# Turning the next stage's first half inside the stage before it, and a feed-forward pipeline that lags by two chunks

## The chip, the cores and the metric

The kernel runs on one core of a Trainium2 chip. The metric is the device time of one launch in microseconds; smaller is better. Float32 data throughout.

## The reference, cut to what matters

256 tokens with 1024 columns go through two blocks and a third part. In each block `h = h + 0.5 * swiglu(rms_norm(h))`, a mixer (attention in two forms in the first block, forgetting attention in the second), a second feed-forward, and a gate:

```python
def swiglu(x, w_gate_up, w_down):
    g, u = jnp.split(x @ w_gate_up, 2, axis=-1)
    return (jax.nn.silu(g) * u) @ w_down
...
    gate = jax.nn.sigmoid(rms_norm(h, ple_norm[i]) @ ple_w_gate[i])
    h = h + gate * (p[i] @ ple_w_proj[i])
```

The third part is block attention and spatial gating, a cross attention on a memory, and a feed-forward over product keys ("peer"), each a norm followed by a product. Every stage thus reads the whole of the `h` that the stage before it has just finished.

## The kernel before, in words

**Arithmetic.** A float32 product is made of three fp32r products, high times high, high times low and low times high (`product`, L248; its matmuls are L250, L251, L252). A stage's input is turned by TensorE (transposes, L255), the high part is cut off the PSUM result by ScalarE (`x_hi`, L277) and the low part by VectorE (`x_lo`, L286, or L289 without a gain). The weights come as 340 units of 1 MB in the order in which they are used (`load_unit`, L223, three places in `raw`, `w_hi` and `w_lo`); ScalarE makes `w_hi` (`split_hi`, L235) and VectorE `w_lo` (`split_lo`, L240). A unit is 24 matmuls of 512 columns: four chunks of 128 rows, two tiles of tokens, three products.

**Order.** There are no queues or planners: each engine runs a program written out by hand (`tensor_program`, L2098, and its siblings), with semaphores between them. An engine works strictly in its order. `split_hi(u + LEAD)` and `split_lo(u + LEAD)` stand beside the use of unit `u`, with LEAD = 2. `split_hi(u)` must wait until TensorE has used unit `u - 3`.

**Stages** are ffa0, mix0 (`tensor_even`), ffb0, ple0, ffa1, mix1 (`tensor_odd`), ffb1, ple1, moba (up to its product out2), cross, peer. The halves below are halves of the 1024 columns of `h`, for all 256 tokens: half 0 is chunks 0 to 3, half 1 chunks 4 to 7. A stage begins like this (`tensor_normed`, `scalar_normed`, `vector_normed`, L319 on):

- TensorE waits for half 0 of `h`, makes 8 transposes, ScalarE makes 4 `x_hi`, VectorE 4 `x_lo`, and the first product waits for the first two of these.
- VectorE adds half 1 of `h` only after these four `x_lo` (the closure `finish`, returned by the stage before: L534 after a feed-forward, L384 after a mixer, L595 and L598 after ple).
- TensorE uses the stage's first unit for token tile 0 (12 matmuls), makes the 8 transposes of half 1, and goes on with token tile 1.
- ScalarE squares all of `h` (L304), POOL makes the root (L314), and only then ScalarE splits the next unit but one.

**A feed-forward** (`tensor_ffn`, L445) has 11 chunks of 256 hidden columns. Of each chunk come two units of first product (`tensor_up`), silu (L476) and times up (`mid`, L507) on ScalarE and VectorE, a turn back (4 transposes, `tensor_back`), `a_hi` (L439) and `a_lo` (L442), and one unit of second product (`tensor_down`) that adds into banks 0 to 3. In TensorE's order the second product of chunk c - 1 stands behind the first of chunk c, and the last stands alone:

```python
    tensor_up(pe, n, c, ffn_up(n, c), free=free, ...)
    tensor_down(pe, n, c - 1, ffn_down(n, c - 1), 2, c == 1, False)
    tensor_back(pe, n, c, 0, lambda c=c: mids(c))
tensor_down(pe, n, NFC - 1, ffn_down(n, NFC - 1), 2, False, True)
```

**ple** (L542) makes the gate's four units, then the small product `p @ w` in one unit; VectorE multiplies and adds (L595, L598).

## Time and profile before

| | |
|---|---|
| device time, 3 runs | median 2199.27 us (2198.82 to 2199.99) |
| the profiled execution, its own time | 2199.95 us |
| its span in the trace | 2198.1 us, 25786 instructions |
| TensorE matmuls (PE) | 2109.9 us, 96%, x10458 |
| TensorE weight loads (PEld) | 1755.1 us, 80% |
| VectorE (DVE), ScalarE (ACT) | 1349.4 us, 61%; 1049.1 us, 48% |
| POOL | 30.7 us, 1% |
| queue of the weights | 426.50 MB, 55.4% of 16 engines |
| mean granted TensorE clock | 0.987 |

A busy TensorE here means that matmuls are in flight; they overlap, and their steps from start to start are shorter than their durations. The span lies 1.85 us below the execution's own time.

### The profile page before, as it was taken

To read this page: it belongs to the slowest core of one execution; us is meant where nothing else is said; L and a number is where in the kernel's file an instruction comes from. 1 tells how busy PE (TensorE), PEld (TensorE's weight loads), DVE (VectorE), ACT (ScalarE), POOL (GpSimd) and SP (SyncE) were. 2 spreads that over 40 slices of the span, in tenths; PEclk is the share of its full clock that TensorE was granted. 3 is DMA by queue.
4 is the path that set the end of the run, shared out by engine and by line. 5 is a ranking of instruction groups with operands and counts; after the bars stand their busy time and mean duration, and the time that the engine had idled before them with its cause. 6 is when DMAs were issued, how large, how long until landed. Compare 5 with 4: busy or idle time off the path is not lost.

```text
span 2198.1 us, 25786 instructions
## 1 busy us (share of the span) xinstructions
PE 2109.9 (96%) x10458; PEld 1755.1 (80%) x10458; DVE 1349.4 (61%) x1789; ACT 1049.1 (48%) x1249; POOL 30.7 (1%) x41
## 2 busy tenths in 40 slices
PE   7999789998999999999999999999999999999997
PEld 6887678887888787788777777888888888888886
DVE  4555764555555565555575655689888746666664
ACT  5444654445444454444557545545545444443442
POOL 1000000000000000000100000000000000000000
PEclk9999999999999998999999999999999999999999
DMA  7554325554455441555543443477699997766772
GB/s 256 188 184 171 134 78 186 184 189 172 155 191 192 153 153 64 175 187 192 195 164 144 153 172 126 163 238 239 230 272 270 277 329 298 282 264 258 264 262 86
DMA packets 95301, 433.73 MB, mean 197 GB/s; under 512 B 7536, under 2 KB 40448, under 8 KB 50384
## 3 DMA queue, kind: packets, MB, share of 16 engines
q1 hardware_dynamic: 93856, 426.50, 55.4%
q0 software_dynamic: 1328, 5.58, 0.8%
q8 instruction: 84, 1.38, 0.2%
q14 instruction: 33, 0.27, 0.0%
HBM read 397.45 MB, written 34.60 MB: 197 GB/s over the span
## 4 chain that ended last, share of the span: by engine, by line
PE 73%; issue 18%; DVE 4%; ACT 4%; DMA 1%; POOL 0%; DVEq 0%; POOLq 0%; SPq 0%; ACTq 0%
PE bank L250 22%; PE bank L252 22%; PE bank L251 22%; PE bank L255 3%; PE bank L1856 2%; DVE w_lo L240 1%; PE bank L693 1%; PE bank L715 1%; ACT w_hi L235 1%; ACT x_hi L277 1%; ACT gated L304 1%; DVE stat L761 0%; DVE x_lo L286 0%; PE bank L1689 0%; DMA parked_a<-one_i 0%
## 5 line engine op out<-in xcount | busy, mean ns | idle before, releaser
L240 DVE TENSOR_TENSOR w_lo<-raw,w_hi 128x2048 fp32r<-128x2048 f32 x340 | 778.9, 2291 | 493.8 <-ACT w_hi L235 493.6
L235 ACT ACTIVATE w_hi<-raw 128x2048 fp32r<-128x2048 f32 x340 | 650.9, 1914 | 634.6 <-PE bank L252 621.7
L250 PE MATMUL bank<-w_hi,x_hi 128*128 128x512 f32 (+1 forms) x2092 | 828.5, 396 | 32.4 <-DVE x_lo L286 13.4
L252 PE MATMUL bank<-w_hi,x_lo 128*128 128x512 f32 (+1 forms) x2092 | 816.0, 390 | 0.0
L251 PE MATMUL bank<-w_lo,x_hi 128*128 128x512 f32 (+1 forms) x2092 | 815.7, 390 | 0.0
L250 PEld LDWEIGHTS bank<-w_hi,x_hi 128*128 128x128 f32 x2092 | 394.8, 189 | 113.9 <-ACT x_hi L277 16.9
L252 PEld LDWEIGHTS bank<-w_hi,x_lo 128*128 128x128 f32 x2092 | 394.8, 189 | 83.1
L251 PEld LDWEIGHTS bank<-w_lo,x_hi 128*128 128x128 f32 x2092 | 395.3, 189 | 77.1
L250 PE MATMUL bank<-w_hi,a_hi 128*128 128x512 f32 x624 | 245.7, 394 | 12.5 <-ACT a_hi L439 5.8
L252 PE MATMUL bank<-w_hi,a_lo 128*128 128x512 f32 x624 | 243.8, 391 | 0.0
L251 PE MATMUL bank<-w_lo,a_hi 128*128 128x512 f32 x624 | 243.8, 391 | 0.0
L250 PEld LDWEIGHTS bank<-w_hi,a_hi 128*128 128x128 f32 x624 | 117.7, 189 | 38.2 <-ACT a_hi L439 6.7
L252 PEld LDWEIGHTS bank<-w_hi,a_lo 128*128 128x128 f32 x624 | 117.7, 189 | 24.8
L251 PEld LDWEIGHTS bank<-w_lo,a_hi 128*128 128x128 f32 x624 | 117.8, 189 | 23.9
L439 ACT ACTIVATE a_hi<-bank 128x512 fp32r<-128x512 f32 x44 | 26.3, 598 | 163.8 <-PE bank L255 163.8
L476 ACT ACTIVATE gated<-bank,small 128x256 f32<-128x256 f32 x88 | 41.8, 475 | 118.3 <-PE bank L252 117.8
L1940 DVE TENSOR_TENSOR gated<-bank,arena 128x512 f32<-128x512 f32 x64 | 65.3, 1061 | 53.4 <-PE bank L255 53.4
L255 PE MATMUL bank<-consts_sb,arena 128*128 128x128 f32 (+2 forms) x566 | 78.4, 277 | 12.6 <-DVE arena L786 5.6
L255 PEld LDWEIGHTS bank<-consts_sb,arena 128*128 128x128 f32 (+2 forms) x566 | 65.5, 138 | 25.9 <-issue 6.8
L442 DVE TENSOR_TENSOR a_lo<-bank,a_hi 128x512 fp32r<-128x512 f32 x44 | 30.4, 692 | 89.3 <-ACT a_hi L439 89.3
L277 ACT ACTIVATE x_hi<-bank,gains_sb 128x256 fp32r<-128x256 f32 x99 | 38.9, 475 | 78.4 <-PE bank L255 78.4
L507 DVE SCALAR_TENSOR_TENSOR mid<-bank,small,gated 128x256 f32<-128x256 f32 x88 | 42.0, 481 | 48.4 <-ACT gated L476 48.4
...
## 6 DMA issues: line engine op xcount, KB each, us to landing
raw<-in_w SPq DMA_DIRECT2D x340, 1024.0 KB, 4.8
...
```

The lines of the kernel that those rows point to most:

```text
L235: act.activation(w_hi[:, u % RING, :, :], raw[:, u % RING, :, :], ACT.Copy).then_inc(*act_done.mark("w_hi", u))
L240: e.tensor_tensor(w_lo[:, u % RING, :, :], raw[:, u % RING, :, :], f32(w_hi[:, u % RING, :, :]), ALU.subtract).then_inc(*dve_done.mark("w_ ...
L250: pe.matmul(out, hi, w_hi[:, s, b, 0:width], start=start, stop=False)
L251: pe.matmul(out, hi, w_lo[:, s, b, 0:width], start=False, stop=False)
L252: return pe.matmul(out, lo, w_hi[:, s, b, 0:width], start=False, stop=stop)
L255: return pe.transpose(out, src, ident[0:src.shape[0], 0:src.shape[0]])
L277: act.activation(hi[:, k, :], bank[b][:, (k - k0) * T:(k - k0 + 1) * T], ACT.Copy, scale=gain_of(k) if gain_of else 1.0).then_inc(*act_don ...
L442: return dve.tensor_tensor(a_lo[:, 2 * b:2 * b + 2, :].rearrange("p f t -> p (f t)"), src, f32(a_hi[:, 2 * b:2 * b + 2, :].rearrange("p f ...
L476: act.activation(gated[:, t, :], bank[GU[t]][:, 0:FC], ACT.Silu, scale=rstd(t)).then_inc(*act_done.mark("silu", n, c, t))
L507: dve.scalar_tensor_tensor(mid[:, t, 0:FC], bank[GU[t]][:, FC:2 * FC], rstd(t), gated[:, t, :], ALU.mult, ALU.mult).then_inc(*dve_done.mar ...
L1856: last = pe.matmul(bank[banks[j // 4]][:, j % 4 * P:(j % 4 + 1) * P], hot_i[:, slot, j // 2, :, j % 2], hot_j[:, slot, 1 + k, j // 2, :, j ...
L1940: dve.tensor_tensor(gated[:, 2 * b:2 * b + 2, :], bank[back_banks(c)[b]][:, :].rearrange("p (f t) -> p f t", f=2), tables[:, piece % N_TAB ...
```

## The change

Each stage's program takes a function `hand`, which does half 0 of the following stage (8 transposes, 4 `x_hi`, 4 `x_lo`) ahead of the last piece of the stage's own last product: ahead of the last unit in mixers, ple and moba; ahead of the last half unit (12 matmuls) in feed-forwards and cross. Half 1 of `h` is added after that piece, and one `split_lo` follows it. In feed-forwards the second product of chunk c - 2 follows the first of chunk c, the turn back of chunk c - 1 stands between the two units of chunk c, and `gated`, `mid`, `a_hi` and `a_lo` alternate between two places; the last two second products run half 0 of both, then half 1 of both. In ple the small product goes first, with half 1's transposes in it. The units are stored and loaded in the new order. The moba-to-cross part also hands over the turns of the keys. No arithmetic is added or left out, and the counts of matmuls, transposes and splits stay. Indentation is cut and some removed lines are left out:

```diff
-plan += [(f"ffb{l}", ffn), (f"ple_gate{l}", units(D, D)), (f"ple_proj{l}", 1)]
+plan += [(f"ffb{l}", ffn), (f"ple_proj{l}", 1), (f"ple_gate{l}", units(D, D))]
...
+stored = list(range(N_UNITS))
+for l in range(DEPTH):
+    p0 = first[f"ple_proj{l}"]
+    stored[p0:p0 + 5] = [p0 + 4] + list(range(p0, p0 + 4))
...
-def tensor_to_h(pe, stage, u0, operand, chunks, ready):
+def tensor_to_h(pe, stage, u0, operand, chunks, ready, hand):
     for n in range(2):
         pair = ((4, 5), (0, 1))[n]
         for i, k0 in enumerate(range(0, chunks, UB)):
             u = u0 + (n * chunks + k0) // UB
+            if n and k0:
+                hand()
             take(pe, u)
             tensor_unit(pe, u, operand, chunks, range(k0, k0 + UB), pair, BLK, ready=ready if n == 0 else None,
+                        between=hand if n and chunks == UB else None,
                         name=(stage, n) if k0 + UB == chunks else None)
+
+def scalar_to_h(act, u0, chunks, hand):
+    last = u0 + 2 * chunks // UB - 1
+    for u in range(u0, last):
+        split_hi(act, u + LEAD)
+    hand()
+    split_hi(act, last + LEAD)
...
-    return first[n] + (3 * c - 1 if c else 0)
+    return first[n] + (2 * c if c < 2 else 3 * c - 2)
 
 def ffn_down(n, c):
-    return first[n] + (3 * c + 4 if c < NFC - 1 else 3 * NFC - 1)
+    return first[n] + (3 * c + 6 if c < NFC - 2 else 2 * NFC + c)
...
+def tensor_down_half(pe, key, c, half):
+    s = ffn_down(key, c) % RING
+    for f in range(2):
+        for t in range(NT):
+            last = product(pe, bank[2 * t + half][:, :], s, 2 * f + half, BLK,
+                           a_hi[:, 2 * (c % 2) + f, t * P:(t + 1) * P], a_lo[:, 2 * (c % 2) + f, t * P:(t + 1) * P],
+                           c == 0 and f == 0, c == NFC - 1 and f == 1)
+    last.then_inc(*pe_done.mark("down", key, c, half))
...
-        tensor_up(pe, n, c, ffn_up(n, c), free=free,
-                  meanwhile=(lambda: tensor_back(pe, n, 0, 0, lambda: mids(0))) if c == 1 else None)
-        tensor_down(pe, n, c - 1, ffn_down(n, c - 1), 2, c == 1, False)
-        tensor_back(pe, n, c, 0, lambda c=c: mids(c))
-    tensor_down(pe, n, NFC - 1, ffn_down(n, NFC - 1), 2, False, True)
+        tensor_up(pe, n, c, ffn_up(n, c), free=free, meanwhile=lambda c=c: tensor_back(pe, n, c - 1))
+        if c >= 2:
+            take_down(pe, n, c - 2)
+            for half in range(2):
+                tensor_down_half(pe, n, c - 2, half)
+            pe_done.also("used", ffn_down(n, c - 2))
+    tensor_back(pe, n, NFC - 1)
+    for half in range(2):
+        for c in (NFC - 2, NFC - 1):
+            if half == 0:
+                take_down(pe, n, c)
+            tensor_down_half(pe, n, c, half)
+            if half == 1:
+                pe_done.also("used", ffn_down(n, c))
+            if half == 1 and c == NFC - 2:
+                hand()
...
         split_hi(act, ffn_up(n, c) + LEAD)
-        if c == 1:
-            hi(0)
         split_hi(act, ffn_up(n, c) + 1 + LEAD)
+        hi(c - 1)
         silu(c)
-        split_hi(act, ffn_down(n, c - 1) + LEAD)
-        hi(c)
+        if c >= 2:
+            split_hi(act, ffn_down(n, c - 2) + LEAD)
+    hi(NFC - 1)
+    split_hi(act, ffn_down(n, NFC - 2) + LEAD)
+    hand()
...
         split_lo(dve, ffn_up(n, c) + LEAD)
-        if c == 1:
-            lo(0)
         split_lo(dve, ffn_up(n, c) + 1 + LEAD)
+        lo(c - 1)
         both(c)
-        split_lo(dve, ffn_down(n, c - 1) + LEAD)
-        lo(c)
+        if c >= 2:
+            split_lo(dve, ffn_down(n, c - 2) + LEAD)
+    lo(NFC - 1)
+    split_lo(dve, ffn_down(n, NFC - 2) + LEAD)
+    vector_acc_to_h(dve, n, n, NFC - 1, 0.5, 0)
+    hand()
+    vector_acc_to_h(dve, n, n, NFC - 1, 0.5, 1)
     split_lo(dve, ffn_down(n, NFC - 1) + LEAD)
...
+PLE_BANKS, PROJ_BANKS, GATE_BANKS = (6, 7, 1, 3), ((4, 5), (0, 2)), ((6, 7), (1, 3))
+
+def tensor_ple(pe, l, prev, hand):
     key, g0, p0 = f"ple{l}", first[f"ple_gate{l}"], first[f"ple_proj{l}"]
...
     take(pe, p0)
     pe.wait_ge(*act_done["ple_a_hi", l])
     pe.wait_ge(*dve_done["ple_a_lo", l])
     for n in range(2):
-        pe.wait_ge(*act_done["ple_gate", l, n, 1])
-        tensor_unit(pe, p0, a_at(), 2, range(2), ((4, 5), (0, 1))[n], BLK, base=2 * n, name=(key, "proj", n))
+        tensor_unit(pe, p0, a_at(2), 2, range(2), PROJ_BANKS[n], BLK, base=2 * n, name=(key, "proj", n))
+        if n == 0:
+            tensor_normed(pe, key, prev, 1, PLE_BANKS)
+    for n in range(2):
+        for i in range(2):
+            u = g0 + 2 * n + i
+            if n and i:
+                hand()
+            take(pe, u)
+            tensor_unit(pe, u, x_at(), KC, range(4 * i, 4 * i + 4), GATE_BANKS[n], BLK,
+                        ready=(lambda k: wait_lift(pe, key, k)) if n == 0 else None, name=(key, n) if i else None)
+
+def scalar_ple_start(act, l, prev):
+    act.wait_ge(p_loaded, 16 * (l + 1))
+    act.wait_ge(*pe_done["used", ffn_down(f"ffb{l}", NFC - 2)])
+    act.activation(a_hi[:, 2:4, :], ple_in, ACT.Copy).then_inc(*act_done.mark("ple_a_hi", l))
+    scalar_normed(act, f"ple{l}", 0, f"ple{l}", prev, PLE_BANKS)
+
+def scalar_ple(act, l, prev, hand):
     key, g0, p0 = f"ple{l}", first[f"ple_gate{l}"], first[f"ple_proj{l}"]
-    for n in range(2):
+
+    def gate(n):
         for t in range(NT):
             act.wait_ge(*pe_done["block", key, n, t])
-            act.activation(ple_gate[:, t, n * BLK:(n + 1) * BLK], bank[((4, 5), (0, 1))[n][t]][:, :], ACT.Sigmoid,
+            act.activation(ple_gate[:, t, n * BLK:(n + 1) * BLK], bank[GATE_BANKS[n][t]][:, :], ACT.Sigmoid,
                            scale=rstd(t)).then_inc(*act_done.mark("ple_gate", l, n, t))
+
     split_hi(act, p0 + LEAD)
+    scalar_normed(act, key, 1, key, prev, PLE_BANKS)
+    split_hi(act, g0 + LEAD)
+    split_hi(act, g0 + 1 + LEAD)
+    gate(0)
+    split_hi(act, g0 + 2 + LEAD)
+    hand()
+    split_hi(act, g0 + 3 + LEAD)
+    gate(1)
+
+def vector_ple_start(dve, l):
+    dve.wait_ge(*act_done["ple_a_hi", l])
+    dve.tensor_tensor(a_lo[:, 2:4, :], ple_in, f32(a_hi[:, 2:4, :]),
+                      ALU.subtract).then_inc(*dve_done.mark("ple_a_lo", l))
+    vector_normed(dve, f"ple{l}", 0, f"ple{l}", PLE_BANKS)
+
+def vector_ple(dve, l, hand):
     key, g0, p0 = f"ple{l}", first[f"ple_gate{l}"], first[f"ple_proj{l}"]
-    finish()
 
     def adds(n):
         for t in range(NT):
             cols = slice(n * BLK, (n + 1) * BLK)
+            dve.wait_ge(*act_done["ple_gate", l, n, t])
             dve.wait_ge(*pe_done["block", key, "proj", n, t])
-            dve.tensor_tensor(ple_gate[:, t, cols], bank[((4, 5), (0, 1))[n][t]][:, :], ple_gate[:, t, cols],
+            dve.tensor_tensor(ple_gate[:, t, cols], bank[PROJ_BANKS[n][t]][:, :], ple_gate[:, t, cols],
                               ALU.mult).then_inc(*dve_done.mark("ple_gated", l, n, t))
             dve.wait_ge(*dve_done["ple_gated", l, n, t])
             dve.tensor_tensor(h[:, t, cols], h[:, t, cols], ple_gate[:, t, cols],
                               ALU.add).then_inc(*dve_done.mark("h", key, n, t))
         dve_done.also("h", key, n)
 
+    split_lo(dve, p0 + LEAD)
+    vector_normed(dve, key, 1, key, PLE_BANKS)
+    split_lo(dve, g0 + LEAD)
+    split_lo(dve, g0 + 1 + LEAD)
     adds(0)
-    return lambda: adds(1)
+    split_lo(dve, g0 + 2 + LEAD)
+    hand()
+    adds(1)
+    split_lo(dve, g0 + 3 + LEAD)
...
-def vector_project_to_h(dve, stage, u0, chunks):
+    vector_project_to_h(dve, "mix1", first["od_out"], KC, hand)
+
+def vector_project_to_h(dve, stage, u0, chunks, hand):
     per = chunks // UB
     for i in range(per):
         split_lo(dve, u0 + i + LEAD)
     vector_to_h(dve, stage, 0)
-    for i in range(per):
+    for i in range(per - 1):
         split_lo(dve, u0 + per + i + LEAD)
-    return lambda: vector_to_h(dve, stage, 1)
+    hand()
+    vector_to_h(dve, stage, 1)
+    split_lo(dve, u0 + 2 * per - 1 + LEAD)
...
+def vector_moba_lift(dve, part):
+    if part == 0:
+        at_mix, at_first = GAINS["mix2"][0], GAINS["final"][0]
+        dve.tensor_tensor(gains[:, at_mix:at_mix + KC], gains[:, at_mix:at_mix + KC], gains[:, at_first:at_first + KC],
+                          ALU.mult).then_inc(*dve_done.mark("both_gains"))
+        dve.wait_ge(*dve_done["both_gains"])
+    for i in (2 * part, 2 * part + 1):
+        vector_lift(dve, "mix2", 2 * i, KC, MIX2_BANKS[i], mix2, x_hi, x_lo)
...
+def tensor_cross_start(pe, prev):
+    tensor_normed(pe, "xa", prev, 0, XA_BANKS)
     for i in (0, 2):
         tensor_turn(pe, "kx", lambda t, x: kn[:, t, x * P:(x + 1) * P], P, i, 2, 6 + i // 2)
...
+    def second_part():
+        pe.wait_ge(*act_done["turned", "kx", 0])
+        pe.wait_ge(*dve_done["turned", "kx", 2])
+        tensor_normed(pe, "xa", prev, 1, XA_BANKS)
...
-    tensor_ffn(pe, "ffa0", None)
+    tensor_normed(pe, "ffa0", None, 0)
+    tensor_ffn(pe, "ffa0", None, lambda: tensor_normed(pe, "mix0", "ffa0", 0))
     pe.wait_ge(more_consts_loaded, 16)
+    tensor_even(pe, "ffa0", lambda: tensor_normed(pe, "ffb0", "mix0", 0))
+    tensor_ffn(pe, "ffb0", "mix0", lambda: tensor_normed(pe, "ple0", "ffb0", 0, PLE_BANKS))
+    tensor_ple(pe, 0, "ffb0", lambda: tensor_normed(pe, "ffa1", "ple0", 0))
+    tensor_ffn(pe, "ffa1", "ple0", lambda: tensor_normed(pe, "mix1", "ffa1", 0, MIX1_BANKS))
+    tensor_odd(pe, "ffa1", lambda: tensor_normed(pe, "ffb1", "mix1", 0))
+    tensor_ffn(pe, "ffb1", "mix1", lambda: tensor_normed(pe, "ple1", "ffb1", 0, PLE_BANKS))
+    tensor_ple(pe, 1, "ffb1", lambda: tensor_moba_lift(pe, "ple1", 0))
+    tensor_moba(pe, "ple1", lambda: tensor_cross_start(pe, "out2"))
+    tensor_cross(pe, "out2", lambda: tensor_normed(pe, "ffn", "cross", 0))
     tensor_peer(pe, "cross")
...
-    parts = [up[:c_up]]
+    parts = [up[:2 * c_up]]
     n = len(up) // c_up
-    for c in range(1, n):
-parts += [up[c * c_up:(c + 1) * c_up], down[(c - 1) * c_down:c * c_down]]
-    return np.concatenate(parts + [down[(n - 1) * c_down:]])
+    for c in range(2, n):
+parts += [up[c * c_up:(c + 1) * c_up], down[(c - 2) * c_down:(c - 1) * c_down]]
+    return np.concatenate(parts + [down[(n - 2) * c_down:]])
```

## Rows read from the trace of the kernel before

**Rows 1.** The page: busy time of the engines, and the chain by engine.

```profile
PE 2109.9 (96%) x10458; PEld 1755.1 (80%) x10458; DVE 1349.4 (61%) x1789; ACT 1049.1 (48%) x1249; POOL 30.7 (1%) x41
...
PE 73%; issue 18%; DVE 4%; ACT 4%; DMA 1%; POOL 0%; DVEq 0%; POOLq 0%; SPq 0%; ACTq 0%
```

**Rows 2.** The chain in two successive feed-forward chunks: start us, us, what.

```profile
63.27 0.44 PE bank L255 x4
...
80.06 0.44 PE bank L255 x4
```

**Rows 3.** What TensorE waited for: us in total, times, longest us.

```profile
PE bank L250 <- DVE x_lo L286: 13.4, 9, 1.6
...
PE bank L250 <- ACT a_hi L439: 5.8, 4, 1.5
...
PE bank L250 <- DVE mid L507: 4.3, 4, 1.1
PE bank L255 <- DVE h L598: 4.3, 2, 2.1
...
PE bank L250 <- ACT f_hi L1139: 1.5, 1, 1.5
```

**Rows 4.** Timeline of TensorE, mix0 to ffb0: start us, us, [idle before].

```profile
321.96 1.03 PE L255 MATMUL bank<-consts_sb,h 128*128 128x128 f32 x8
324.49 0.47 PE L250 MATMUL bank<-w_hi,x_hi 128*128 128x512 f32 x1 [1.49 <-DVE x_lo L286]
...
327.33 1.03 PE L255 MATMUL bank<-consts_sb,h 128*128 128x128 f32 x8
...
337.61 0.47 PE L250 MATMUL bank<-w_hi,x_hi 128*128 128x512 f32 x1 [1.06 <-DVE mid L507]
```

**Rows 5.** Timeline of TensorE at the end of ffa0.

```profile
197.45 0.60 PE L255 MATMUL bank<-consts_sb,mid 128*128 128x128 f32 x4
199.51 0.47 PE L250 MATMUL bank<-w_hi,a_hi 128*128 128x512 f32 x1 [1.46 <-ACT a_hi L439]
```

**Rows 6.** Timeline of TensorE from ple0 to ffa1.

```profile
546.33 1.28 PE L255 MATMUL bank<-consts_sb,h 128*128 128x128 f32 x8 [2.13 <-DVE h L598]
548.91 0.76 PE L250 MATMUL bank<-w_hi,x_hi 128*128 128x512 f32 x1 [1.30 <-DVE x_lo L286]
```

**Rows 7.** Two stretches: start:end, us, busy of PE, PEld, DVE, ACT, POOL; clock, DMA.

```profile
548.90:554.05 5.15, 5.14 (x12) 4.00 (x13) 5.08 (x7) 1.48 (x1) 0.00 (x0) 0.51 0.00 0
1110.20:1114.65 4.45, 4.40 (x12) 3.48 (x13) 4.38 (x7) 1.46 (x1) 0.00 (x0) 0.62 0.00 0
```

**Rows 8.** Timeline of TensorE at the start of cross.

```profile
1313.77 1.10 PE L255 MATMUL bank<-consts_sb,h 128*128 128x128 f32 x8 [0.34 <-ACT arena L627]
```

**Rows 9.** Timeline of ScalarE, mix0 to ffb0.

```profile
327.97 1.57 ACT L277 ACTIVATE x_hi<-bank,gains_sb 128x256 fp32r<-128x256 f32 x4 [2.00 <-PE bank L255]
...
332.76 1.92 ACT L235 ACTIVATE w_hi<-raw 128x2048 fp32r<-128x2048 f32 x1 [1.00 <-POOL small L314]
```

**Rows 10.** Timeline of VectorE, mix0 to ffb0.

```profile
323.47 1.66 DVE L286 SCALAR_TENSOR_TENSOR x_lo<-bank,gains_sb,x_hi 128x256 fp32r<-128x256 f32 x4 [2.45 <-ACT x_hi L277]
325.04 1.28 DVE L384 TENSOR_TENSOR h<-bank,h 128x512 f32<-128x512 f32 x2
...
334.78 2.29 DVE L240 TENSOR_TENSOR w_lo<-raw,w_hi 128x2048 fp32r<-128x2048 f32 x1 [2.82 <-ACT w_hi L235]
336.99 0.87 DVE L507 SCALAR_TENSOR_TENSOR mid<-bank,small,gated 128x256 f32<-128x256 f32 x2
...
348.44 0.48 DVE L507 SCALAR_TENSOR_TENSOR mid<-bank,small,gated 128x256 f32<-128x256 f32 x1
```

**Rows 11.** Timeline of ScalarE and VectorE at the end of ple0.

```profile
538.79 0.69 ACT L572 ACTIVATE arena<-bank,small 128x512 f32<-128x512 f32 x1 [2.03 <-PE bank L252]
...
549.47 0.68 DVE L595 TENSOR_TENSOR arena<-bank,arena 128x512 f32<-128x512 f32 x1
...
550.18 0.69 DVE L598 TENSOR_TENSOR h<-h,arena 128x512 f32<-128x512 f32 x1
```

300 lines of the change are left out of this document (113 added, 187 removed).

## The prediction, made before the change was run

> **What bounds the kernel now.** I read the page first: TensorE has matmuls in flight 96% of the span, VectorE and ScalarE are busy 61% and 48%, and the chain that ended last is 73% TensorE [rows 1]. So the time is TensorE's steps plus the places where it stands still. Second, the chain inside a feed-forward: from one turn back to the next it takes 80.06 - 63.27 = 16.79 us [rows 2]. Without the 0.44 us of transposes that is 16.35 us for 72 products, 0.227 us each, with no room for a wait; a unit of 24 costs 5.45 us, half a unit 2.73. Third, the list of TensorE's waits [rows 3], which says where it does stand still: for `x_lo` at nine stage starts, and at the tenth (mix1) booked on `f_hi`; four times for `a_hi`; twice for the last sums of ple; four times for `mid`. Together 13.4 + 1.5 + 5.8 + 4.3 + 4.3 = 29.3 us, 1.3% of the time. That is nearly all this change can aim at. Fourth, the timelines around these places, for what each wait is made of.
>
> **The price of each wait before.** From start to start, since the durations overlap.
> - A handover: transposes start at 321.96, the first product at 324.49 [rows 4], 2.53 us. Eight transposes take 0.87 of it at their step of 0.11 us (twice the 0.44 of four, rows 2), so 1.66 stand idle. The products after it need 327.33 - 324.49 = 2.84 where half a unit is 2.73, another 0.11. Ten handovers: 17.7 us.
> - The last second product of a feed-forward: 199.51 - 197.45 = 2.06, less 0.44, is 1.62 [rows 5]. Four times: 6.5 us.
> - At the end of ple TensorE stands idle 2.13 us by the row, 2.3 from start to start, before it may turn `h` at all [rows 6]; the wait list has it twice [rows 3]. 4.6 us.
> - Behind ple the clock falls. The 12 products after 548.91 take 5.15 us at a granted clock of 0.51, and those after 1110.25 take 4.45 at 0.62 [rows 7], against 2.73: 2.4 + 1.7 = 4.1 us at the lower of the two levels (1.2 GHz, the steps being near 0.43 us). What the engine did before: within some 5 us it made eight transposes and waited twice [rows 6]. Single waits of 1.5 us [rows 4, 5] were followed by full speed.
> - In cross, 0.34 us idle for the turned keys, about 0.4 with the step [rows 8].
>
> Sum: 17.7 + 6.5 + 4.6 + 4.1 + 0.4 = 33.3 us.
>
> **What the change makes of them.** Let E be the moment when TensorE begins the new stage's first unit. Half 0 is turned at E - 3.6 (behind feed-forwards and before peer) or E - 6.3. ScalarE starts 0.64 us after the transposes (327.33 to 327.97, rows 4 and 9), the first `x_lo` pair is ready 2.4 us after them (321.96 to 324.49 with the product, less 0.15) and the fourth after 3.2 (323.47 + 1.66 - 321.96, rows 4 and 10). So all is ready by E - 0.4 at the latest, and the 1.66 + 0.11 go everywhere. Half 0 of `h` must be summed by E - 3.6: in a feed-forward the second halves of the last two products leave 2.73 us for two adds of 1.28 together [rows 10], and in mixers and ple a whole unit, 5.45 us, lies between. The `a_hi` wait goes because the product of chunk 9 stands over it (half 0: 2.73 us against 1.62 idle).
>
> The work that covered VectorE's later steps is thinner now. Behind E it has, in order: the rest of half 1's sum, one `split_lo` that stood ahead of E before, the next `split_lo`, then the `x_lo` of half 1. A `split_lo` costs 2.29, 2.21 with the overlap of its neighbours (334.78 to 336.99, rows 10). TensorE wants `x_lo` at E + 2.73 + 0.87 + 2.73 = E + 6.33; two of them with the wake-up take 1.0 us.
> - Feed-forward to mixer: sum done at E + 0.4 + 1.28 = 1.7; two splits and a small operation, 6.15; product at 7.1. **New wait 0.8** in mix0; 0.95 in mix1, whose `f_lo` comes first.
> - Mixer to feed-forward, and moba to cross: only one add of 0.69 is left behind E, 1.1; splits to 5.5; product at 6.45. **0.1**.
> - ple to ffa1 and to moba: sigmoid 0.69 from E + 0.2, product 0.68, add 0.69 [rows 11]: 2.3; splits to 6.7; product at 7.7. **1.4** each.
> - Feed-forward to ple: the small product (5.45 us in all) stands between, the first product on half 1 comes at E + 11.8. **None.** Cross to peer **0.1**.
>
> Then the wait for `mid` at chunk 1. Its chain is squares, root, `split_hi`, `split_lo`, `mid`, product; before it ends at 337.61 - 324.49 = 13.12 behind the first product [rows 4, 10]. After, ScalarE's squares end at E + 3.4 + 3.8 = 7.2 (327.97 to 332.76 less the 1.00 idle, rows 9). Behind a mixer `x_lo` is done by 7.1, so the chain ends at E + 12.9, no later than before. In ffa1 the mean must wait for the last `x_lo` at 8.3, which puts it at E + 14.1, 1.0 later. That 1.0 contains what is left of ffa1's 1.4. So the new cost is 0.8 + 0.95 + 1.0 + 1.4 + 0.1 = 4.3 us, and I take off 0.2 for the three `mid` chains that end a little sooner: **4.1 us**.
>
> The lag of two adds no instruction. Its own new risk is chunk 2: the first product of chunk 2 now follows chunk 1 directly, and wants `mid` of chunk 1. Before, that `mid` is done at 348.44 + 0.48 = 348.92 [rows 10], while chunk 1's products end at 337.61 + 48 x 0.227 + 0.44 + 0.1 = 349.05. `split_hi` now comes ahead of `a_hi` there, `a_lo` behind the split instead of ahead of it, which moves `mid` by -0.2 to +0.2. I cost it at **0**; with no cover left it would be 0.2 each, 0.8. Later chunks have a unit of second product over it. DMAs: every unit is loaded as before, but the load behind the moved `split_lo` starts up to 6 us later; it is wanted more than 20 us behind E, so 0. POOL's queue keeps its order.
>
> **Sum:** 33.3 - 4.1 = 29.2 us; 0.4 for the first products behind the four new waits gives **28.8 us**. Of the profiled execution's 2199.95 this leaves 2171.2; the median of the three runs lies 0.7 below it, so 2170.5.
>
> **A rule against it.** The slow stretch behind ple [rows 7] is what I count back in full. The Trainium skill, TensorE: Matmul & The Clock Gate, Part 4 (PE-mode transpose), says that transposes do not count as work for the clock as products do. By that rule the hand-in transposes lengthen the thin places that are left: in ffa1 and moba 0.87 us of them, then a wait. Products stand between in both, and no row here shows a fall behind a single wait; by the row the sum is 2170.5, by the rule it may be rival 1.
>
> **Rivals.**
> 1. *The clock still falls behind ple.* Two waits remain in ffa1 (1.4, then about 0.7). If the lower level is granted to 12 products behind them, the 4.1 us stay: 2174.6. For it: waits stay there. Against: about 5.5 us of products lie between them, where before there were only transposes. 0.07.
> 2. *The lag or the splits cost more than worked out.* Each of eight starts waits one `split_lo` (2.21 us) longer, because ScalarE or VectorE comes late by a turn, or chunk 2 waits for `mid` as chunk 1 does (1.06 by rows 4, four times). 4 to 18 us lost: 2175 to 2188, middle 2180. For it: VectorE's order behind E is full without a gap. Against: ScalarE has idle time in the same stretch [rows 9]. 0.13.
> 3. *Slower.* TensorE's clock falls at each place where it still waits, ten starts and four `mid` waits. Each fall costs up to 2.4 us (rows 7), 14 of them 34 us against 28.8: 2204. It decides from 12 falls on. The single waits before are as long and made none. 0.02.
> 4. *The change does not do what it says*, because half 0 of `h` is late and TensorE waits inside the last product instead of behind it: 2190 to 2200, median 2197. The margins of 1.1 us and more speak against it. 0.04.
>
> My forecast has 0.74.
>
> **How the numbers follow.** The forecast's own bounds: no new wait at all gives 33.3, 2166; each new wait twice as long gives 2174.6. The range 2165.5 to 2179 takes in rival 1 and half of rival 2, leaving about 0.15 outside. What a measurement here can tell from no change is about 0.2%, 4.4 us. Faster by more than that: the forecast, rivals 1 and 2 and half of rival 4, 0.95; same 0.03; slower 0.02.
>
> **What would show it.** `a_hi` and the h wait of ple gone from TensorE's list; the wait for `x_lo` down from 13.4 to about 5 us, at four starts, with w_lo just ahead of it on VectorE; no step of 0.43 us behind ple; chunk period 16.8 us unchanged; `mid` still four times near 1.1. Wrong would be: waits for `h` inside a stage's last product, a fifth to eighth `mid` wait at chunk 2, or slow products at a stage start.

## The result, and the profile after

The changed kernel takes **2173.14 us** (median), the kernel before, run beside it, 2199.56. The ratio of the two is 0.9875, with a 95% interval of 0.9861 to 0.9888. The profiled execution took 2173.41 us with a span of 2171.6. I predicted 2170.5 with a range of 2165.5 to 2179.0. The median is over four executions; one of them took 9418 us and is in no ratio, and the other three have a median of 2172.88 us (2168.41 to 2173.41).

The page of the changed kernel: busy time of the engines, and the chain by engine.

```profile
PE 2105.5 (97%) x10458; PEld 1753.9 (81%) x10458; DVE 1345.4 (62%) x1789; ACT 1048.8 (48%) x1249; POOL 30.7 (1%) x41
...
PE 74%; issue 18%; DVE 5%; ACT 3%; DMA 1%; POOL 0%; DVEq 0%; POOLq 0%; SPq 0%; ACTq 0%
```

Against [rows 1] the counts of every engine's instructions are the same, so what changed is their order. TensorE's busy share rose from 96 to 97% because idle time left the span.

The list of TensorE's waits (us in total, times, longest us). The lines moved: products are now L255 to L257, transposes L260, `x_lo` L291, `mid` L515.

```profile
PE bank L255 <- DVE w_lo L245: 6.4, 1, 6.4
...
PE bank L255 <- DVE mid L515: 3.9, 4, 1.1
...
PE bank L255 <- DVE x_lo L291: 3.3, 4, 1.2
```

Beside [rows 3]: `x_lo` fell from 13.4 us at nine places to 3.3 at four; `a_hi`, `h` and `f_hi` are gone; `mid` stayed at four places. The 6.4 us for `w_lo` are the first stage's, 6.3 before. Those are the places of the forecast; for `x_lo` it had about 5 us in this list, and 3.3 came.

The timeline of TensorE at the end of ffa0 and the start of mix0 (start us, us, what, idle before).

```profile
201.38 1.03 PE L260 MATMUL bank<-consts_sb,h 128*128 128x128 f32 x8
202.17 0.47 PE L255 MATMUL bank<-w_hi,a_hi 128*128 128x512 f32 x1
...
205.02 0.39 PE L255 MATMUL bank<-w_hi,x_hi 128*128 128x512 f32 x1
...
207.75 1.03 PE L260 MATMUL bank<-consts_sb,h 128*128 128x128 f32 x8
...
211.92 0.47 PE L255 MATMUL bank<-w_hi,x_hi 128*128 128x512 f32 x1 [0.40 <-DVE x_lo L291]
```

The eight transposes of half 0 stand 3.64 us ahead of the first product on `x_hi` (205.02), the forecast E - 3.6, and nothing is idle ahead of that product. In [rows 4] such a pair, at the next stage, had 1.49 us idle between them. What remains is the forecast new wait at half 1. VectorE in the same stretch shows how it is made:

```profile
205.22 1.29 DVE L548 SCALAR_TENSOR_TENSOR h<-bank,h 128x512 f32<-128x512 f32 x2 [0.67 <-PE bank L257]
206.43 2.28 DVE L245 TENSOR_TENSOR w_lo<-raw,w_hi 128x2048 fp32r<-128x2048 f32 x1
...
208.70 2.29 DVE L245 TENSOR_TENSOR w_lo<-raw,w_hi 128x2048 fp32r<-128x2048 f32 x1
210.90 1.65 DVE L291 SCALAR_TENSOR_TENSOR x_lo<-bank,gains_sb,x_hi 128x256 fp32r<-128x256 f32 x4
```

The sum of half 1, two splits, `x_lo`: the product starts at E + 6.90, where I had E + 7.1. Of the step from the product before it, 211.13 to 211.92, 0.56 us is wait (forecast 0.8).

Behind ple, where [rows 7] show a granted clock of 0.51 and 0.62, the windows of the changed kernel over the end of ple0, the wait (1.18 us idle in the timeline) and the products behind it, then behind the same wait in moba (us; PE, PEld, DVE, ACT, POOL; clock, DMA share, GB/s) read:

```profile
540.40:543.15 2.75, 2.75 (x18) 2.40 (x17) 2.75 (x2) 2.09 (x5) 0.00 (x0) 1.00 0.00 0
543.80:545.40 1.60, 0.42 (x3) 0.05 (x1) 1.60 (x4) 1.05 (x2) 0.00 (x0) 1.00 0.94 369
545.40:548.10 2.70, 2.70 (x12) 2.26 (x13) 0.69 (x3) 1.21 (x1) 1.93 (x4) 1.00 1.01 404
...
1093.20:1096.00 2.80, 2.72 (x12) 2.29 (x13) 1.96 (x4) 1.36 (x1) 0.72 (x1) 1.00 1.02 418
```

The granted clock is 1.00, the upper of the two levels (2.4 GHz), in all four. Twelve products take 2.7 to 2.8 us, where they took 5.15 and 4.45.

**Where the time came from.** I took the same product, by its place in TensorE's order, in both traces, and the difference of its starts, at a point inside each stage. The difference grows by:

| up to | forecast, us | measured, us |
|---|---|---|
| ffa0, its start | 0 | -0.74 |
| mix0 | 1.62 + 1.77 - 0.8 = 2.59 | 2.85 |
| ffb0 | 1.77 - 0.1 = 1.67 | 1.68 |
| ple0 | 1.62 + 1.77 = 3.39 | 3.45 |
| ffa1, behind chunk 1 | 2.3 + 1.77 + 2.4 - 1.0 = 5.47 | 5.39 |
| mix1 | 1.62 + 1.77 - 0.95 = 2.44 | 2.65 |
| ffb1 | 1.67 | 1.89 |
| ple1 | 3.39 | 3.38 |
| moba, first unit | 2.3 + 1.77 + 1.7 - 1.4 = 4.37 | 4.36 |
| the rest of moba | 0 | -2.12 |
| cross and peer | 1.67 + 0.4 + 1.67 = 3.74 | 3.73 |
| sum | 28.7 | 26.5 |

The rows where the change acts agree within 0.26 us each, and their sum, 29.4 us, is 0.7 above the 28.7 forecast. The two rows that it does not touch, the first products of ffa0 and the rest of moba, lost 2.9 us. Of the 2.12 us in moba, 1.6 are in one place of its attention; the same 15 products before and after take 1.3 us longer, and the four small ones just ahead 0.3:

```profile
1161.16:1164.69 3.53, 3.53 (x18) 2.90 (x17) 0.86 (x2) 2.50 (x6) 0.00 (x0) 1.00 0.00 0
1136.58:1141.38 4.80, 4.80 (x18) 3.83 (x17) 1.70 (x3) 2.61 (x5) 0.00 (x0) 0.72 0.00 0
```

The other 0.5 are two more products at the doubled step behind a wait of 3.47 us that both kernels have (1252.42 before, 1229.12 after).

### The profile page after: what moved, and what is told of

Same layout as the page of the kernel before. It is cut to its first block, busy times and chain, and to the rows that moved or that the text cites. A ratio compares the mean times of both kernels' runs of the same rounds, so it can differ in the third digit from the quotient of the medians.

```text
span 2171.6 us, 25749 instructions
## 1 busy us (share of the span) xinstructions
PE 2105.5 (97%) x10458; PEld 1753.9 (81%) x10458; DVE 1345.4 (62%) x1789; ACT 1048.8 (48%) x1249; POOL 30.7 (1%) x41
## 4 chain that ended last, share of the span: by engine, by line
PE 74%; issue 18%; DVE 5%; ACT 3%; DMA 1%; POOL 0%; DVEq 0%; POOLq 0%; SPq 0%; ACTq 0%
PE bank L255 22%; PE bank L257 22%; PE bank L256 22%; PE bank L260 3%; PE bank L1891 2%; DVE w_lo L245 2%; PE bank L720 1%; PE bank L742 1%; ACT w_hi L240 1%; ACT x_hi L282 1%; ACT gated L309 0%; DVE stat L788 0%; DMA parked_a<-one_i 0%; PE bank L1724 0%; DVE arena L813 0%
## 5 line engine op out<-in xcount | busy, mean ns | idle before, releaser
L255 PE MATMUL bank<-w_hi,x_hi 128*128 128x512 f32 (+1 forms) x2092 | 827.1, 395 | 20.4 <-DVE w_lo L245 6.4
L257 PE MATMUL bank<-w_hi,x_lo 128*128 128x512 f32 (+1 forms) x2092 | 815.7, 390 | 0.0
L255 PEld LDWEIGHTS bank<-w_hi,x_hi 128*128 128x128 f32 x2092 | 394.5, 189 | 101.6 <-issue 8.4
L257 PEld LDWEIGHTS bank<-w_hi,x_lo 128*128 128x128 f32 x2092 | 394.2, 188 | 82.4
L256 PEld LDWEIGHTS bank<-w_lo,x_hi 128*128 128x128 f32 x2092 | 394.8, 189 | 76.9
L255 PE MATMUL bank<-w_hi,a_hi 128*128 128x512 f32 x624 | 246.5, 395 | 6.7 <-DVE a_lo L294 3.5
L257 PE MATMUL bank<-w_hi,a_lo 128*128 128x512 f32 x624 | 244.1, 391 | 0.0
L255 PEld LDWEIGHTS bank<-w_hi,a_hi 128*128 128x128 f32 x624 | 117.9, 189 | 31.3 <-ACT a_hi L282 3.7
L257 PEld LDWEIGHTS bank<-w_hi,a_lo 128*128 128x128 f32 x624 | 117.8, 189 | 24.8
L260 PE MATMUL bank<-consts_sb,arena 128*128 128x128 f32 (+2 forms) x566 | 78.2, 276 | 12.8 <-DVE arena L813 6.0
L260 PEld LDWEIGHTS bank<-consts_sb,arena 128*128 128x128 f32 (+2 forms) x566 | 65.3, 138 | 25.8 <-issue 6.7
L515 DVE SCALAR_TENSOR_TENSOR mid<-bank,small,gated 128x256 f32<-128x256 f32 x88 | 41.9, 479 | 45.1 <-ACT gated L484 45.1
L1881 DVE TENSOR_TENSOR arena<-arena 128x1024 bf16<-128x1024 bf16 x96 | 60.5, 686 | 0.0
L291 DVE SCALAR_TENSOR_TENSOR x_lo<-bank,gains_sb,x_hi 128x256 fp32r<-128x256 f32 x99 | 41.1, 477 | 30.7 <-ACT x_hi L282 30.5
```

The costliest lines, as they stand in the source:

```text
L255: pe.matmul(out, hi, w_hi[:, s, b, 0:width], start=start, stop=False)
L256: pe.matmul(out, hi, w_lo[:, s, b, 0:width], start=False, stop=False)
L257: return pe.matmul(out, lo, w_hi[:, s, b, 0:width], start=False, stop=stop)
L260: return pe.transpose(out, src, ident[0:src.shape[0], 0:src.shape[0]])
L515: dve.scalar_tensor_tensor(mid[:, t, c % 2 * FC:(c % 2 + 1) * FC], bank[GU[t]][:, FC:2 * FC], rstd(t), gated[:, 2 * (c % 2) + t, :], ALU.mult,
L1881: last = dve.tensor_tensor(hot_j[:, slot, 1 + k, :, :, :], hot_j[:, slot, 0, :, :, :], token_cols(2 + k), ALU.mult)
```

## Experiments

All ratios are against the kernel before, run on the same chip; I compare variants with the changed kernel repeated, 2172.08. Not all ran on its chip; the kernel before had medians of 2199.34 to 2199.97 beside them.

### The changed kernel again

No edit.

> The changed kernel once more, unchanged. Its profiled execution took 2173.4 us, its other runs 2168.4 and 2172.9. My account: the stage starts gave what was forecast, and what lies between one execution and another is where the granted clock falls at the start, in the attention stages and nowhere else. So the waits of TensorE repeat within 0.1 us each, the time is 2168 to 2174, and a faster execution has fewer products at the 0.43 us step. Rival: the spread comes from waits on weights or on DMA; then the list of waits differs between executions by 4 us.

Measured: **2172.08 us** (2171.01 to 2173.14), ratio 0.9877 [0.9861, 0.9894]. Its waits at stage starts and in feed-forwards are those of the first trace within 0.1 us; some in the attention differ by up to 0.7. Its trace is 28.9 us ahead of the kernel before at the last product, against 26.5 for the first. The 2.3 us between two executions of one program are 1.0 at the first products (8 of them took the slower step instead of 12) and 2.1 in the attention of mix1, less 0.8 lost in that of mix0.

### The handover undone

At the end of each stage, on all three engines, behind the last product; in feed-forwards:

```diff
+            split_lo(dve, ffn_down(n, NFC - 1) + LEAD)
             vector_acc_to_h(dve, n, n, NFC - 1, 0.5, 0)
             hand()
             vector_acc_to_h(dve, n, n, NFC - 1, 0.5, 1)
-            split_lo(dve, ffn_down(n, NFC - 1) + LEAD)
```

> Only the handover is undone: half 0 of the next stage is turned and split behind the last piece again, and half 1's sum follows it with the split ahead of it, as before. The lag of two and the new order of ple stay. If the handover is what gives most: eight stage starts get 1.77 us back (14.2; the two starts of ple no longer need half 0 at once, and in cross the turned keys cover 0.9 of it), and the new waits at the starts go (3.6), so +9.7 us against the changed kernel, about 2182.5; with slow products behind ple again up to 2186.5. Rival (the lag of two and ple's new order give nearly all): 2172 to 2175.

Measured: **2199.48 us** (2198.28 to 2206.06), ratio 1.0009 [1.0, 1.0019]. The whole gain was gone, 27.4 us where I had expected some 10. TensorE's waits (us in total, times, longest), and then TensorE and VectorE at the end of ffa0:

```profile
PE bank L260 <- DVE h L544: 12.1, 5, 2.9
PE bank L255 <- DVE x_lo L291: 9.5, 7, 1.7
```

```profile
206.05 1.97 PE L260 MATMUL bank<-consts_sb,h 128*128 128x128 f32 x8 [2.87 <-DVE h L544]
209.09 0.77 PE L255 MATMUL bank<-w_hi,x_hi 128*128 128x512 f32 x1 [1.08 <-DVE x_lo L291]
...
202.50 2.29 DVE L245 TENSOR_TENSOR w_lo<-raw,w_hi 128x2048 fp32r<-128x2048 f32 x1 [5.47 <-ACT w_hi L240]
204.71 1.28 DVE L544 SCALAR_TENSOR_TENSOR h<-bank,h 128x512 f32<-128x512 f32 x2
```

My variant had a wait of its own. With a lag of two both last second products give their weights free only in their second halves, so the last split on VectorE waits 5.47 us for `w_hi`, and I had put the sum of half 0 behind it. The products that follow ran at the slow step (8 of them from 209.1, 11 behind the end of ffa1, 6 behind that of ffb1, none behind ffb0). This run therefore says nothing on the size of the handover; it shows that one split ahead of the sum of `h` costs a wait of 2.9 us in each feed-forward.

### Only TensorE's part of the handover undone

```diff
-                    if half == 1 and c == NFC - 2:
-                        hand()
+            hand()
```

and likewise in mixers, ple and moba; ScalarE's and VectorE's orders stay.

> The changed kernel with TensorE's part of the handover undone alone: at every stage it turns half 0 of the next stage's input behind its last product instead of between the last ones; the orders of ScalarE and VectorE, the lag of two and the order in ple are kept (the variant before that undid the handover had its last split ahead of the sum of half 0 on VectorE, so TensorE waited up to 2.9 us for h, a wait of its own). Theory A: the handover is worth the 17.7 us that I gave it: 10 places at 1.66 and 0.11; the sums of half 0 are ready when TensorE ends, so no wait for h; half 1's x_lo comes 0.2 to 0.5 later than now: 2191 us (2188 to 2195), x_lo in TensorE's list near 18. Theory B: most of the gain is the lag of two and ple's order, and the handover brings little: below 2183. Theory C: where a handover's idle time and a second wait follow each other the clock falls again: each of these is 1.3 to 2.5 more, above 2196 in sum.

Measured: **2192.3 us** (2191.06 to 2194.25), ratio 0.9968 [0.9956, 0.998].

```profile
PE bank L255 <- DVE x_lo L291: 17.6, 15, 1.6
...
PE bank L260 <- DVE h L614: 3.7, 2, 1.9
...
PE bank L255 <- DVE mid L512: 3.2, 4, 1.1
...
PE bank L260 <- DVE h L545: 1.3, 2, 0.6
```

Theory A, with one miss. The `x_lo` waits come back, 17.6 - 3.3 = 14.3 us of idle, and 5.0 us for `h` that I had said would not be there: 3.7 of them for half 1 of `h` in ffa1 and moba, whose sum now stands behind the late `x_lo` of half 0 on VectorE. From transposes to product a handover takes 2.53 us again (543.66 to 546.19 at ffa1), exactly as in [rows 4]. Eight starts have such a wait, 1.2 to 1.6 us idle each, 11.8 us in sum; the two ples have none, since their small product now goes first and covers it. The rest of the 20.2 us between this run and the changed kernel comes with it, in helper engines whose order was made for the early turn: the waits for half 1, in `x_lo` and `h`, stand in the list above.

### A lag of one with the handover kept

```diff
+            return first[n] + (3 * c - 1 if c else 0)
-            return first[n] + (2 * c if c < 2 else 3 * c - 2)
...
+                take_down(pe, n, c - 1)
...
+            tensor_down_half(pe, n, NFC - 1, 0)
+            tensor_down_half(pe, n, NFC - 1, 1, hand)
```

> Only the feed-forward lag is undone: second products follow by one chunk, the last one stands alone, and the handover lies in its last quarter, 6 matmuls ahead of the stage's end. My theory: four times 1.62 us for a_hi, about 0.6 for h and 0.2 for x_lo come back (9.7), and the two waits for x_lo behind feed-forwards go (1.25): +8.4, about 2181.5. Rival (the lag is worth nothing, because the a_hi wait has another cover): 2171 to 2175. Second rival: the handover needs the lag to work at all; then TensorE waits 2 us or more for h at each feed-forward's end, and the time is 2186 or more.

Measured: **2176.86 us** (2176.18 to 2181.41), ratio 0.9904 [0.9888, 0.9921].

```profile
PE bank L255 <- DVE a_lo L519: 6.0, 4, 1.5
...
PE bank L255 <- DVE mid L511: 3.9, 4, 1.1
...
PE bank L255 <- DVE x_lo L291: 2.3, 2, 1.2
```

The wait at a feed-forward's end is back, 6.0 us at four places, as [rows 3] had it with 5.8; 1.0 us of `x_lo` went the other way. The run as a whole is only 4.8 us slower, where I had expected 8.4, and its time alone lies between that and the rival of no effect. The table of the mixers' attention below accounts for most of the difference: outside it the run is 8.0 us behind the changed kernel repeated.

### The end of ple as before

```diff
-            adds(0)
             split_lo(dve, g0 + 2 + LEAD)
-            hand()
-            adds(1)
             split_lo(dve, g0 + 3 + LEAD)
+            dve.wait_ge(*pe_done["block", key, 1, 1])
+            adds(0)
+            hand()
+            adds(1)
```

TensorE's and ScalarE's handover stands behind the last gate unit as well.

> The changed kernel with the end of the two ple stages as before the change: half 0 of h is summed only behind the last gate unit, and half 0 of the next stage is turned behind that; all else is kept. Theory A: TensorE stands idle for h (2.3 us) and for x_lo (1.8 us) at the start of ffa1 and of moba, 8.2 us in all, and behind that idle the clock falls to its lower level as in the kernel before (4.1 us more): 2184 us (2181 to 2187), with 10 or more product steps of 0.43 us behind each ple. Theory B: the slow clock behind ple was not made by that idle: the idle comes back and all steps are 0.227 us: 2180 us (2178 to 2181).

Measured: **2181.54 us** (2180.17 to 2182.94), ratio 0.992 [0.9907, 0.9934]. The timeline of TensorE, and two windows behind ple:

```profile
539.80 1.57 PE L260 MATMUL bank<-consts_sb,h 128*128 128x128 f32 x8 [2.83 <-DVE h L617]
542.45 0.77 PE L255 MATMUL bank<-w_hi,x_hi 128*128 128x512 f32 x1 [1.07 <-DVE x_lo L291]
```

```profile
542.40:548.20 5.80, 5.75 (x19) 4.68 (x20) 5.54 (x7) 1.77 (x2) 0.00 (x0) 0.59 0.01 1
1093.80:1098.70 4.90, 4.90 (x20) 4.02 (x21) 4.83 (x7) 1.50 (x2) 0.00 (x0) 0.71 0.00 0
```

The clock is down again in both places, 0.59 and 0.71, and nowhere else behind a stage start; the products at the doubled step cost 2.3 and 1.5 us (11 and 7 of them). That is theory A: the slow stretch belongs to this idle. The kernel with TensorE's part undone makes the contrast in the same stage: TensorE waited 1.50 us for `x_lo`, 1.92 for `h` and 1.44 for `x_lo` again, each time with products in between, and the windows behind the second and third wait show full clock:

```profile
551.00:553.70 2.70, 2.62 (x16) 2.32 (x17) 2.70 (x3) 1.93 (x5) 0.00 (x0) 1.00 0.00 0
556.30:559.10 2.80, 2.74 (x12) 2.33 (x13) 0.77 (x3) 1.23 (x1) 1.95 (x4) 1.00 1.03 415
```

### Half 1's `x_lo` and mean ahead of a split

The first split behind E goes behind `x_lo` and the mean at every stage start:

```diff
-            split_lo(dve, ffn_up(n, 0) + LEAD)
-            vector_normed(dve, n, 1, n)
+            vector_normed(dve, n, 1, n, then=lambda: split_lo(dve, ffn_up(n, 0) + LEAD))
```

> VectorE's order behind the handover is changed at the stage starts (feed-forwards, mix0, mix1, moba, cross, peer): half 1's x_lo and the mean come ahead of the next split_lo instead of behind it. If the new waits for x_lo come from that split_lo, they go from 3.3 us (four times) to under 0.5, mix0, mix1 and moba gain 0.55, 0.7 and 1.35, ffa1 1.1 over both its waits: 2169 for the execution that takes 2173 now, -3.9 us. Rival (the x_lo wait is bounded by ScalarE's x_hi or by the sum of half 1): no change, 2172 to 2174. Second rival: the split_lo comes late for its own unit and TensorE waits for w_lo instead: 2173 or more, with w_lo in the list of waits beyond the first stage's 6.4 us.

Measured: **2183.7 us** (2183.26 to 2184.74), ratio 0.993 [0.9913, 0.9946]; 11.6 us slower than the changed kernel. That is neither my forecast nor a rival of mine: it is slower, but TensorE does not wait for `w_lo` beyond the first stage. The wait for `x_lo` was gone, but that for `mid` was 12.2 us at four places instead of 3.9. VectorE, then ScalarE, then GpSimd at the start of ffb0:

```profile
329.98 0.17 DVE L314 TENSOR_SCALAR small<-small 128x2 f32<-128x2 f32 x1 [1.29 <-ACT gated L309]
330.06 2.28 DVE L245 TENSOR_TENSOR w_lo<-raw,w_hi 128x2048 fp32r<-128x2048 f32 x1
...
332.93 1.92 ACT L240 ACTIVATE w_hi<-raw 128x2048 fp32r<-128x2048 f32 x1 [2.97 <-POOL small L319]
...
330.23 2.66 POOL L319 TENSOR_TENSOR small<-small,consts_sb 128x2 f32<-128x2 f32 x1 [89.12 <-DVE small L314]
```

The same in the changed kernel:

```profile
328.00 0.17 DVE L314 TENSOR_SCALAR small<-small 128x2 f32<-128x2 f32 x1 [0.32 <-ACT gated L309]
...
328.25 0.69 POOL L319 TENSOR_TENSOR small<-small,consts_sb 128x2 f32<-128x2 f32 x1 [88.35 <-DVE small L314]
...
328.98 1.92 ACT L240 ACTIVATE w_hi<-raw 128x2048 fp32r<-128x2048 f32 x1 [1.00 <-POOL small L319]
330.91 1.28 ACT L484 ACT_TABLE_LOAD   x1
332.21 1.07 ACT L484 ACTIVATE gated<-bank,small 128x256 f32<-128x256 f32 x2
...
333.20 0.87 DVE L515 SCALAR_TENSOR_TENSOR mid<-bank,small,gated 128x256 f32<-128x256 f32 x2
```

The root of two numbers a row takes 0.69 us on GpSimd when VectorE is idle, and 2.66 when a split runs beside it; it ends 0.55 us after that split (332.34 and 332.89). ScalarE waits for it, and `mid` behind ScalarE. The Trainium skill, SBUF — State Buffer, section "SBUF: two separate sides", says that GpSimd shares a pair of ports with VectorE, and that an operation on VectorE with two inputs in SBUF, against one on GpSimd that reads SBUF, holds it to its end if it starts first, while the other is blocked wholly. The rows agree: the split reads `raw` and `w_hi`, the root reads `small`, started 0.17 us later and ended behind it. A GpSimd operation that only writes was not held up: in the kernel of 2167.24 us further down, clearing `arena` (128x2048) took 1.84 us, from 25.98 to 27.82, with splits on VectorE from 24.84 to 29.33. Two more orders test this.

### The split between `x_lo` and the mean

```diff
             if part:
+                if then:
+                    then()
                 vector_mean(dve, key, D, 0)
```

> The changed kernel with half 1's x_lo ahead of one weight split on VectorE and the mean behind that split, the gate of chunk 0 left where it was: what stands between the kernel of 2183.7 us (x_lo and mean both ahead) and that of 2160.8 (x_lo ahead and the gate early). Theory A: the 11 us lost there came from the mean, which waits for ScalarE's squares and keeps the split idle behind it. With the mean behind the split the wait for x_lo (3.3 us) goes nearly whole, the chain to mid starts up to 1 us later, so the wait for mid grows from 3.9 to at most 8: 2169 to 2175 us, middle 2172. Theory B: the late split itself lost the time, and what saved the kernel of 2160.8 was the early gate alone: 2180 or more, with the wait for mid at 11 or more. What in the kernel of 2160.8 came from fewer products at the lower clock in the attention of the mixers (4 of its 6.3 us) is not in either number.

Measured: **2172.77 us** (2171.87 to 2174.17), ratio 0.9877 [0.986, 0.9893]. The number is that of theory A, but not yet its reason: the order ends two things at once, the split that idles behind the mean and the split that runs over the root. The mean starts behind the split and the root takes 0.69 us again. `x_lo` is no longer waited for, `mid` grew from 3.9 to 7.9 us: one wait was exchanged for the other, since VectorE is full in this stretch and the chain to `mid` starts one split later.

### The split behind the root

```diff
                 vector_mean(dve, key, D, 0)
                 dve.wait_ge(*pool_done["rstd", key])
+                if then:
+                    then()
```

> The kernel of 2183.7 us (x_lo and mean of half 1 ahead of a weight split on VectorE) with one step moved: that split now waits until GpSimd's root is done. In the trace of that kernel the root, 0.69 us in the changed kernel, takes 2.66 (from 330.23, while the split runs on VectorE from 330.06 to 332.34), and ScalarE and with it mid wait behind it. Theory A: the two engines cannot work on these operands at the same time; what cost 11 us was the split over the root. Kept apart, the root is back to 0.69 us in every row, the wait for mid falls from 12.2 to between 4 and 7 us, and the time is 2170 us (2167 to 2174). Theory B: the split that comes late lost the time by itself (it is 1 us later still here): 2180 or more, mid at 11 or more.

Measured: **2167.24 us** (2165.7 to 2168.57), ratio 0.9853 [0.9838, 0.9868]. It differs from the kernel of 2183.7 us in nothing but that the split waits for the root (at every stage start but moba's, where it stayed over it), is later by that, and the kernel is 16 us faster. The wait for `mid` is 5.1 us. Nine of the 17 places of the root took 2.6 us or more in the kernel of 2183.7 us, and one, moba's, does here; the median of the row is what it takes alone (the first row is this kernel, the second that of 2183.7 us; shortest, median, longest):

```profile
L319 POOL TENSOR_TENSOR small<-small,consts_sb x17: 688/695/2686, 24.1 to 2156.3; 128x2 f32<-128x2 f32 x17
```

```profile
L319 POOL TENSOR_TENSOR small<-small,consts_sb x17: 688/2597/2692, 24.5 to 2173.8; 128x2 f32<-128x2 f32 x17
```

So it was the split over the root, not the late split. Nor was it the reason that I had given in the run before, a split kept idle behind the mean: here it is idle for longer. The gain was even 3 us more than expected.

### The gate of chunk 0 ahead of a split

The rows of ScalarE in the changed kernel above show where `mid` is late: a split (1.92 us), a table load (1.28 us) and only then the gate (332.21), though the first half of its products was ready near 330.

```diff
-            split_hi(act, ffn_up(n, 0) + 1 + LEAD)
-            silu(0)
+            silu(0, lambda: split_hi(act, ffn_up(n, 0) + 1 + LEAD))
...
-            split_lo(dve, ffn_up(n, 0) + 1 + LEAD)
             both(0)
+            split_lo(dve, ffn_up(n, 0) + 1 + LEAD)
```

> The changed kernel with one step moved, in the four feed-forwards alone: the gate of chunk 0's first token half is taken ahead of the weight split that stood before it on ScalarE, and both products of chunk 0 ahead of that unit's second split on VectorE. Theory A: the wait for mid behind a feed-forward's start (3.9 us in all four) is ScalarE's: behind the squares it makes a split (328.98 to 330.89), loads the table of the gate function (330.91 to 332.19), and only then the first gate (332.21), though its products were ready at about 330. With the split behind the first gate mid comes some 1.9 us earlier and the wait is gone: 2168.5 us (2167 to 2170), mid gone from TensorE's list, the wait for x_lo still 3.3. Theory B: the wait hangs on the mean and its root, which nothing here moves, or the split that is now late makes TensorE wait for w_lo or a_lo instead: 2172 or more.

Measured: **2167.14 us** (2165.82 to 2167.68), ratio 0.9852 [0.9836, 0.9867]. `mid` has left TensorE's list, `x_lo` stands at 3.3, no new wait came. Theory A: the wait for `mid`, which the kernel had before the change too, comes from the helpers' order. How much of it is ScalarE's split and how much VectorE's (331.00 to 333.29 in the changed kernel, with `mid` right behind it) is not separated, since the edit moves both.

### Both orders together

> As the run before it, and at each stage start half 1's x_lo goes ahead of one of the two weight splits on VectorE, the mean behind that split (where x_lo and the mean both went ahead of it, 2183.7 was measured). Theory A: that run lost because the mean waits for ScalarE's squares and kept the split behind it on VectorE idle; with the split between x_lo and the mean nothing is kept idle, x_lo comes about 1 us earlier, its wait (3.3 us) falls to 1 or less and mid has slack to bear a mean that is 1 us later: 2166 us (2164.5 to 2169). Theory B: what lost there was the late split itself, on which the chain of splits hangs (load, first part, second part, next load): then waits for mid or w_lo grow here too and the time is above 2172.

Measured: **2160.83 us** (2160.53 to 2165.69), ratio 0.9832 [0.9818, 0.9845]. That is 5 us faster than theory A had it; the next section says where most of it is.

> The run before it with the gate of chunk 0 taken early as well, so that neither x_lo nor mid is waited for behind a stage's start. Against the kernel of 2160.8 us (x_lo, split, mean) the mean comes up to 1 us earlier and the split 1 to 3 us later. Theory A: no wait is left that either order could take away, so the two are equal but for the clock in the mixers' attention: 2158 to 2167 us, with no wait for x_lo or mid in TensorE's list. Theory B: the later split makes TensorE wait for w_lo, or ScalarE and VectorE late for the next chunk: 2168 or more.

Measured, with the split behind the root: **2158.68 us** (2158.13 to 2164.56), ratio 0.9819 [0.9805, 0.9832]. It lies in theory A's range. Neither `x_lo` nor `mid` is left in TensorE's list of these stages in either. The two are equal within what a measurement tells. Both beat the changed kernel, the second by 13.4 us of median: it is the fastest kernel of this study.

### What the mixers' attention adds to every comparison

Removing 3.3 us of waits from the kernel of 2167.14 gave 6.3. The rest is in stretches whose instructions are the same in all kernels here. The windows between the same two products around mix0's attention, the first of the kernel of 2167.14 us, the second of that of 2160.83:

```profile
244.43:300.84 56.41, 46.70 (x263) 39.72 (x263) 43.46 (x143) 33.18 (x116) 0.00 (x0) 0.83 0.11 38
```

```profile
244.11:297.19 53.08, 42.81 (x262) 36.38 (x263) 43.38 (x143) 33.29 (x116) 0.00 (x0) 0.91 0.11 40
```

The same attention runs at a mean granted clock of 0.83 in one trace and 0.91 in the other, which is, by my estimate from these means, some 19 and 10 us at the lower level. For every trace I took the time between the same two products around the attention of mix0, mix1 and moba, and what is left of the span without them:

| kernel | mix0 | mix1 | moba | span without the three |
|---|---|---|---|---|
| before | 53.7 | 79.2 | 122.3 | 1942.9 |
| changed | 53.7 | 79.1 | 123.9 | 1914.9 |
| changed, again | 54.5 | 76.9 | 123.9 | 1914.0 |
| handover undone | 53.8 | 79.1 | 122.3 | 1941.3 |
| TensorE's part undone | 56.7 | 76.4 | 122.3 | 1935.3 |
| lag of one | 53.1 | 77.0 | 122.3 | 1922.0 |
| ple as before | 54.6 | 76.4 | 123.9 | 1924.9 |
| `x_lo` and mean ahead | 54.5 | 79.1 | 122.2 | 1925.8 |
| split between them | 56.6 | 76.4 | 122.3 | 1917.1 |
| split behind the root | 53.8 | 76.9 | 122.3 | 1911.3 |
| gate early | 56.4 | 79.1 | 122.3 | 1908.1 |
| gate early, split between | 53.1 | 76.4 | 122.3 | 1906.9 |
| gate early, split behind the root | 54.5 | 76.3 | 122.3 | 1905.7 |

mix0 spreads over 3.6 us and mix1 over 2.9; moba has two values 1.6 us apart. The upper one stands in both traces of the changed kernel and in that with the old end of ple, and in no other, though the early gate edits nothing in moba and has the lower one: whether the changed order brings it or chance is not settled. In the last column the change is worth 28.0 us (28.9 for the repeat), against a forecast of 28.8; the lag of two 7.6 rather than 4.8; the two new orders on top of the early gate 1.2 and 2.4.

## Why the prediction was right, and by how much it missed

- **What bounds the kernel.** Right. TensorE's plain steps did not change; nearly all that moved was its idle time and the stretches at the lower clock, and the table above has each place of [rows 3] within 0.26 us of its cost.
- **The price of a handover, 1.66 + 0.11.** Right: 1.68 us in ffb0, where nearly nothing else changes. Undoing TensorE's part brought back the step of 2.53 us between transposes and product, at eight starts. I had counted ten: the two of ple are won by its small product, which now goes first, and need no early turn.
- **The end of a feed-forward, 1.62.** Right: 3.45 us in ple0 against 3.39, where a handover is in both numbers, and 6.0 us of idle at four places when the lag was one.
- **The end of ple, 2.3, and the clock behind it, 4.1.** Right: 5.39 and 4.36 us against 5.47 and 4.37, and putting the old end of ple back brought the slow products back at the same two places.
- **The new waits, 4.1.** The mechanism, two splits ahead of `x_lo` on VectorE, was right at all four starts. From start to start they are 0.56 us in mix0, 0.69 in mix1 and 1.34 each in ffa1 and moba, for 0.8, 0.95 and 1.4 forecast. `mid` is waited for 3.9 us in four places instead of 4.3. Chunk 2 waits for nothing, as costed.
- **The sum itself.** It takes the new wait of 0.1 once, though I had costed it at four starts (ffb0, ffb1, cross, peer), which is 0.3 more; by places the forecast is 28.7 only because the 0.4 for first products and the 0.2 for `mid` are not in it. The three all but cancel, and that is luck.
- **The step that missed: "no change" where nothing is edited.** The median lies 2.6 us above the forecast. The first products of ffa0 (0.7 us) and the rest of moba (2.1) are slower in the profiled execution than before, on the same instructions: in moba at a lower granted clock, in ffa0 by products at the doubled step (12 where 8 were), though the window over them (14.59:20.59) reads a granted clock of 1.00. The sum had no term for this, and my range took it in only because it was wide for other reasons. Part of it was made up for by the places that gave 0.7 us more than costed. The second execution of the same kernel had 1.0 of it back at the start and 2.1 in mix1, and lost the same 1.6 in moba.
- **Rivals.** 1 did not come: no slow product stands behind ple. The Trainium skill, TensorE: Matmul & The Clock Gate, Part 4 (PE-mode transpose), whose rule stood behind it, is neither shown nor excluded: with products on both sides of the transposes and waits of 1.34 us and less at stage starts, no fall came. 2 did not come in this kernel; the kernel with `h` behind a split shows what such an order costs, 2.9 us at each feed-forward's end. 4 is excluded by the list of waits, in which TensorE waits for `h` at no stage's end, and 3 by the time and by a granted clock of 1.00 behind the longest new waits.
